# Down-projection of a ConvFFN: nine tiles by twenty-two rows of weights, or seven block products with accumulating DMAs

## The reference

```python
h = jnp.einsum('btd,de->bte', x, w_in)
# gMLP on chunks of 128, and sliding-window attention -> mix (width 1024)
mix = jnp.einsum('bte,ed->btd', mix, w_out)
x = layer_norm(DEEPNORM_ALPHA * x + mix, ln1_g, ln1_b)

up = jnp.einsum('btd,df->btf', x, w_up)                  # 1024 -> 2 * 2816
hp = jnp.concatenate([conv_prefix, up], axis=1)
hc = conv_b + sum(conv_w[i] * hp[:, i:i + T] for i in range(CONV_WIDTH))
g, u = hc[..., :D_FF], hc[..., D_FF:]
y = jnp.einsum('btf,fd->btd', jax.nn.gelu(g, approximate=False) * u, w_down)
x = layer_norm(DEEPNORM_ALPHA * x + y, ln2_g, ln2_b)
```

## Time and profile before

| | us |
|---|---|
| median of three runs | 2283.82 |
| profiled execution, span | 2283.5 |
| TensorE busy | 2185.3 (96%) |
| VectorE busy | 1651.1 (72%) |
| ScalarE busy | 981.5 (43%) |
| GpSimd busy | 832.3 (36%) |
| up-projection of a layer, by the trace | 421.5 |
| down-projection of a layer, by the trace | 268.4 |

### The profile page before, as it was taken

One profiled execution on the slowest core, in us unless ns is written; L12 is line 12 of the kernel. 1 busy time (PEld: TensorE's weight loads), 2 busy tenths in 40 slices (PEclk: granted clock), 3 DMA queues, 4 the chain that ended last, 5 costly groups with the idle time before them and its releaser, 6 DMA issues.

```text
span 2283.5 us, 35524 instructions
## 1 busy us (share of the span) xinstructions
PE 2185.3 (96%) x14132; PEld 1986.4 (87%) x14132; DVE 1651.1 (72%) x2004; ACT 981.5 (43%) x1767; POOL 832.3 (36%) x444
## 2 busy tenths in 40 slices
PE   7999999899999999999999999989999999999996
PEld 7997677799999998888899876779999999988885
DVE  1477767878788886787636687677777878867677
ACT  3226755544344434343422276464434443443342
POOL 1115255554554450320311242446455445311311
PEclk9999999999999999999999999999999999999998
DMA  6303166223322325665562122641332233365762
GB/s 157 86 20 84 33 206 175 65 58 86 88 69 77 86 69 203 235 213 195 193 140 48 48 51 87 179 152 51 83 86 77 69 88 86 98 250 185 241 217 92
DMA packets 208766, 269.74 MB, mean 118 GB/s; under 512 B 31953, under 2 KB 167377, under 8 KB 208529
## 3 DMA queue, kind: packets, MB, share of 16 engines
q1 hardware_dynamic: 208600, 267.46, 39.2%
HBM read 217.65 MB, written 46.13 MB: 116 GB/s over the span
## 4 chain that ended last, share of the span: by engine, by line
PE 76%; DVE 14%; ACT 5%; issue 3%; POOL 2%; DMA 0%; SPq 0%; ACTq 0%; DVEq 0%; POOLq 0%
PE ps L2153 37%; PE ps L1872 17%; PE ps L1831 9%; PE ps L2092 5%; DVE bnst L1292 1%; PE ps L1897 1%; DVE rl L1491 1%; PE ps L1976 1%; DVE rzc L1278 1%; PE ps L1955 1%; DVE cb L1564 1%; POOL bl L762 1%; PE ps L1991 1%; DVE Sb L1610 1%; PE ps L2002 1%
## 5 line engine op out<-in xcount | busy, mean ns | idle before, releaser
L2153 PE MATMUL ps<-bt,bh 128*128 128x272 f32 (+1 forms) x3520 | 591.1, 290 | 18.7 <-DVE bt L1397 9.3
L2153 PEld LDWEIGHTS ps<-bt,bh 128*128 128x128 f32 x3520 | 503.3, 190 | 20.3 <-DVE bt L1397 9.7
L979 ACT ACTIVATE bh<-wblk 128x512 fp32r<-128x512 f32 x308 | 183.6, 624 | 483.1 <-POOL wblk L774 268.2
L2153 PE MATMUL ps<-bt,bl 128*128 128x272 f32 (+1 forms) x1760 | 369.1, 290 | 0.0
L2153 PEld LDWEIGHTS ps<-bt,bl 128*128 128x128 f32 x1760 | 278.4, 190 | 0.0
L762 POOL TENSOR_TENSOR bl<-wblk,bh 128x512 fp32r<-128x512 f32 x98 | 168.4, 1721 | 283.8 <-ACT bh L979 283.8
L1872 PE MATMUL ps<-rh,ah 128*128 128x512 f32 x792 | 245.6, 391 | 4.6 <-DVE ah L1502 3.2
L1872 PE MATMUL ps<-rl,ah 128*128 128x512 f32 x792 | 244.1, 389 | 0.0
L2153 PE MATMUL ps<-ba,bh 128*128 128x272 f32 (+2 forms) x1408 | 233.8, 288 | 4.0 <-DVE gu L1438 2.4
L1415 DVE TENSOR_TENSOR bl<-wblk,bh 128x512 fp32r<-128x512 f32 x210 | 169.0, 837 | 91.7 <-ACT bh L979 91.7
L1491 DVE TENSOR_TENSOR rl<-wrow,rh 128x1024 fp32r<-128x1024 f32 x132 | 189.5, 1437 | 42.5 <-ACT rh L1035 42.3
(11 more groups left out here) (222 smaller groups left out, 4042.3 us busy)
## 6 DMA issues: line engine op xcount, KB each, us to landing
wrow<-in_w_down SPq DMA_DIRECT2D x132, 512.0 KB, 4.8
wblk<-in_w_up SPq DMA_DIRECT2D x88, 512.0 KB, 5.3
a_scr<-hg SPq DMA_DIRECT2D x44, 552.0 KB, 3.5
araw<-a_scr SPq DMA_DIRECT2D x88, 192.0 KB, 4.4
wrow<-in_w_out SPq DMA_DIRECT2D x48, 256.0 KB, 5.1
wrow<-in_w_out SPq DMA_DIRECT2D x24, 512.0 KB, 4.2
wraw<-in_w_in SPq DMA_DIRECT2D x10, 1024.0 KB, 6.3
z_scr<-rzc SPq DMA_DIRECT2D x16, 512.0 KB, 4.6
```

The lines of the kernel that those rows point to most:

```text
L979: act.activation(bh[b][:], block_of(f, b), ACT.Copy).then_inc(S["u_hi"], 1)
L2153: e = nc.tensor.matmul(up_half(f, b, n), lhs, rhs[:, c:HW_] if n else rhs[:, 0:c], start=(k == 0 and m == 0), stop=(k == HK - 1 and m == 2))
```

## The change

The down-projection becomes seven block products too. The 2816 inner rows are split by parity of their 128-row block (even blocks are "1", odd ones "2"), the output columns into two halves of 512, the prompt tokens into tiles 0..3 and 4..7. Seven products (`P_1, P_2, P_3, P_6, P_5, P_7, P_4`, in that order of time) of 11 steps each, NST = 77 steps in all; a step has one 128 x 512 block of weights or of a sum of weights, one 128 x 512 block of activations or of a sum, and four token tiles in four PSUM banks. The 64 samples are not part of that: for them four ordinary block products go along with P_1, P_2, P_3 and P_5, two matmuls a step.

- Sums of activations are made in the up-projection, in device memory: ScalarE writes the negated first half of `hg` (`negated`, behind `tap_up`), SyncE stores it to `e_scr` and `f_scr` (`neg_out`), and GpSimd adds to it by accumulating DMAs, of 512, 512 and 256 KB for each pair of steps (`act_add`).
- Sums of weights: blocks of `w_down` are held whole in SBUF (`w11`, `w12`, `w21`, `w22`); ScalarE negates one (`weight_neg`) and GpSimd accumulates the other onto it from device memory (`weight_add`), 12 DMAs of 0.75 to 1 MB in a layer.
- Residual rows and gains: scaled by GpSimd (`residual`), the bias row, the first product and the partial sums then accumulated by DMAs (`residual_add`, seven in a layer, of 0.25 to 2 MB); for six tiles the second layer norm's last addition is an accumulating DMA too (`gained` of GpSimd).
- Joins: VectorE adds each finished bank to the rows in SBUF (`join`, `second`, `sample_part`).
- The buffers `hg[0]` and `hg[1]` are read by those DMAs, and `tap_gate` waits for them.
- In the second layer the input projection's chunks are 512, 288 and 288 columns instead of 384, 384 and 320, and tiles 4 to 7 are transposed there instead of 6 to 8.

The core of the diff:

```diff
@@ constants
+KP = FT // 2
+NP = 7
+NST = NP * KP
+P_1, P_2, P_3, P_6, P_5, P_7, P_4 = range(NP)
+PX, PY, PZ = [6, 7, 2, 5], [3, 4, 0, 1], [2, 5, 6, 7]
+KGRP = [(0, 4), (4, 8), (8, KP)]
+X_AT = {62: 0, 64: 1, 68: 2, 70: 3, 72: 8}
@@ SyncE
+            def neg_out(l, k, which):
+                sp.wait_ge(S["neg"], neg_a(l, k, which) + 1)
+                if which == 0:
+                    sp.dma_start(e_scr[k, :, 0:3:2, :], hx[:, 0:1, :].to_broadcast([P, 2, HT])).then_inc(S["e_out"], 16)
+                else:
+                    sp.dma_start(f_scr[k], hx[:, 1, :]).then_inc(S["f_out"], 16)
...
                 sp.dma_start(a_scr[f], hg[f % 2][:]).then_inc(S[f"a_out{f % 2}"], 16)
+                if f % 2 == 0:
+                    sp.dma_start(e_scr[f // 2, :, 1, :], hg[0][:, HT:2 * HT]).then_inc(S["a_out0"], 16)
...
+                    if f >= 2:
+                        neg_out(l, f // 2 - 1, f % 2)
...
+                for s in range(4, NST):
...
+                    elif s in (14, 16):
+                        if s == 14:
+                            sp.wait_ge(S["adds1"], 16 * KP * (l + 1))
+                        z_back(l, s // 2 - 3 + (s - 14) // 2)
+                        z_back(l, s // 2 - 2 + (s - 14) // 2)
...
+                    elif s == 17:
+                        down_block(l, "w22", 0, 0, KP)
...
+                    act_block(l, s)
@@ GpSimd
+            def act_add(l, k, i):
+                n = l * KP + k
+                if i == 0:
+                    pool.wait_ge(S["e_out"], 16 * (n + 1))
+                    pool.dma_start(e_scr[k, :, 0:3:2, :], hg[0][:, HT:2 * HT].unsqueeze(1).to_broadcast([P, 2, HT]),
+                                   accum_op=ALU.add).then_inc(S["adds0"], 16)
+                elif i == 1:
+                    pool.wait_ge(S["prod"], l * FT + 2 * k + 2)
+                    pool.wait_ge(S["a_out0"], 32 * (n + 1))
+                    pool.wait_ge(S["adds0"], 16 * (n + 1))
+                    pool.dma_start(e_scr[k, :, 1:3, :], hg[1][:, HT:2 * HT].unsqueeze(1).to_broadcast([P, 2, HT]),
+                                   accum_op=ALU.add).then_inc(S["adds1"], 16)
+                else:
+                    pool.wait_ge(S["f_out"], 16 * (n + 1))
+                    pool.wait_ge(S["adds1"], 16 * (n + 1))
+                    pool.dma_start(f_scr[k], e_scr[k, :, 2, :], accum_op=ALU.add).then_inc(S["adds2"], 16)
+            def weight_add(l, which, g):
+                k0, k1 = KGRP[g]
+                tile, block, c = {T_1: (w11, 0, HT), T_2: (w22, 1, HT), T_3: (w12, 0, HT), T_4: (w21, 1, 0)}[which]
+                pool.wait_ge(S["neg"], neg_t(l, which, g) + 1)
+                after(pool, f"wadd{g}", 16 * (4 * l + which))
+                src = w_down[l].rearrange("(k two p) n -> two p k n", two=2, p=P)[block][:, k0:k1, c:c + HT]
+                pool.dma_start(tile[:, k0:k1, :], src, accum_op=ALU.add).then_inc(S[f"wadd{g}"], 16)
...
                 for f in range(1, FT):
                     lo_up(l, f, B_11)
                     lo_up(l, f, B_12)
-                    for b in SUMS:
+                    for b in SUMS[:3]:
                         sum_up(l, f, b)
+                    sum_up(l, f, B_S3)
+                    if f >= 5 and f % 2:
+                        act_add(l, (f - 5) // 2, 2)
+                    if f >= 3 and f % 2:
+                        act_add(l, (f - 3) // 2, 0)
+                    elif f >= 4:
+                        act_add(l, (f - 4) // 2, 1)
@@ ScalarE
             def tap_gate(l, f):
                 n = l * FT + f
                 act.wait_ge(S["up_in"], n + 1)
                 if f >= 2:
-                    act.wait_ge(S[f"a_out{f % 2}"], 16 * (l * (FT // 2) + f // 2))
+                    if f % 2:
+                        act.wait_ge(S["a_out1"], 16 * (l * KP + f // 2))
+                        act.wait_ge(S["adds1"], 16 * (l * KP + f // 2))
+                    else:
+                        act.wait_ge(S["a_out0"], 32 * (l * KP + f // 2))
+                        act.wait_ge(S["adds0"], 16 * (l * KP + f // 2))
...
+            def negated(l, k, which):
+                act.wait_ge(S["prod"], l * FT + 2 * k + which + 1)
+                after(act, ("adds0", "f_out")[which], 16 * (l * KP + k))
+                act.activation(hx[:, which, :], hg[which][:, 0:HT], ACT.Copy, scale=-1.0).then_inc(S["neg"], 1)
...
                     tap_gate(l, f)
                     tap_up(l, f)
+                    if f:
+                        negated(l, (f - 1) // 2, (f - 1) % 2)
+                for s in range(NST):
+                    if s + 2 < NST:
+                        down_hi(l, s + 2)
+                        act_hi(l, s + 2)
...
+                    elif 58 <= s < 63:
+                        if s < 62:
+                            deviation2(l, TOP[s - 58])
+                        if s == 61:
+                            deviation2(l, NB)
+                        normal2(l, TOP[s - 58])
@@ TensorE
+                    for m, (lhs, rhs) in enumerate(((lh_, rh_), (lh_, rl_), (ll_, rh_))):
+                        e = nc.tensor.matmul(ps[:, P_BANKS[p][i], :], lhs, rhs, start=(fresh and m == 0), stop=(final and m == 2))
...
+                    for m, rhs in enumerate((dh[s % 3], dl[s % 3])):
+                        e = nc.tensor.matmul(ps[:, P_SAMP[p], :], smp[:, f, :], rhs[:], start=(k == 0 and m == 0),
+                                             stop=(k == KP - 1 and m == 1))
```

More of the change, by code:

```diff
@@ L1073, in body @@
                 else:
-                    for t in G3[2]:
+                    for t in range(4, NB):
                         x_hi(l, t)
@@ new lines, in sample_part @@
+            def sample_part(l, n, half, bank):
+                k = JOINS * l + (J_S1 + (0 if half else 2), J_S2, J_S3, J_S5)[n]
+                dve.wait_ge(S["d_samp"], 4 * l + n + 1)
+                rz = half_of(NB, half)
+                dve.wait_ge(S["radd"], 16 * (RADDS * l + R_8))
+                if n:
+                    dve.wait_ge(S["joins"], JOINS * l + {1: J_S1 + 4, 2: J_S1 + 2, 3: J_S3 + 2}[n])
+                for i in range(2):
+                    if i:
+                        dve.wait_ge(S["joins"], k + 1)
+                    dve.tensor_tensor(rz, rz, ps[NS * i:NS * i + NS, bank, :], ALU.add).then_inc(S["joins"], 1)
@@ new lines, in second, with stats @@
+            def second(l, i):
+                dve.wait_ge(S["d_tile"], 4 * (l * NP + P_6) + i + 1)
+                dve.wait_ge(S["radd"], 16 * (RADDS * l + R_P1))
+                dve.tensor_tensor(p1[:, i, :], p1[:, i, :], ps[:, PY[i], :], ALU.add).then_inc(S["joins"], 1)
+            def stats(l, t, half):
+                q = tokens(t)
+                if t == NB:
+                    dve.wait_ge(S["joins"], JOINS * l + (J_S5 if half else J_S2) + 2)
+                else:
+                    j = (J_VT if half else J_C11) if t < 4 else J_C22 if half else J_C21
+                    dve.wait_ge(S["joins"], JOINS * l + j + t % 4 + 1)
+                dve.bn_stats(out=bst[0:q, t, 6 * half:6 * half + 6], in_=half_of(t, half)).then_inc(S["ln_bn"], 1)
@@ new lines, in body @@
+                    if l < DEPTH - 1 and s in X_AT:
+                        x_lo(l + 1, X_AT[s])
+                for t in (4, 5):
+                    join(l, J_C21, t - 4)
+                    stats(l, t, 0)
+                    moments2(l, t)
+                scaled2(l, 4)
+                scaled2(l, 5)
+                dve.wait_ge(S["gain_landed"], 64 * (l + 1))
+                gained(l, 4)
+                for t in (6, 7):
+                    join(l, J_C21, t - 4)
+                    stats(l, t, 0)
+                    moments2(l, t)
@@ new lines, in down_step @@
+                def down_step(s, tiles=(0, 1, 2, 3)):
+                    p, k = divmod(s, KP)
+                    if p in P_SAMP and k == KP - 1:
+                        down_samples(s)
+                    for i in tiles:
+                        down_tile(s, i)
+                    if p in P_SAMP and k < KP - 1 and 3 in tiles:
+                        down_samples(s)
+                down_ready(0)
+                down_step(0, (0, 1))
+                down_ready(1)
+                down_step(1, (0, 1))
@@ new lines, in body @@
+                for s in range(2):
+                    down_step(s, (2, 3))
+                for s in range(2, NST - 3):
+                    down_ready(s)
+                    down_step(s)
+                    if s == 4:
+                        rows_turn(NRB - 1)
+                    if l < DEPTH - 1 and s in X_AT:
+                        turn_x(l + 1, X_AT[s])
+                for tiles in ((0, 1), (2, 3)):
+                    for s in range(NST - 3, NST):
+                        down_ready(s)
+                        down_step(s, tiles)
```

899 lines of the change are left out of this document (593 added, 306 removed), and 2 rows, old and new, of the table S.

## The result

The changed kernel takes 2560.86 us (median of four runs, 2555.66 to 2561.84), the kernel before 2283.23 beside it: the ratio is 1.120, with a 95% interval of 1.118 to 1.122. The forecast was 2358 with a range to 2450. The direction was right, the size was not: 278 us more instead of 74. The page of the kernel after, to be read beside the earlier trace rows: span, busy times, two of the DMA queues (q0 holds the transfers issued by GpSimd, the accumulating ones among them), and the chain that ended last.

What follows compares the result with a forecast made beforehand. TensorE was taken to bound both stages, with the gate tap's new wait binding the up-projection after the change: 2283.5 - 60 + 108 + 26 = 2357.5, with 0.3 us for the median 2358 us, range 2245 to 2450.

Steps and rivals of the forecast that it cites:

- Matmuls, -60 us: Down-projection: 1012 matmuls a layer instead of 1144, at 0.2268 us each, 29.9 us a layer less on TensorE.
- a few hundredths: TensorE's granted clock in the up-projection: the most it was expected to fall, hidden because TensorE no longer bounds the loop.
- The wait of the gate tap, +108 us: Up-projection: 19 taps a layer wait for an accumulating DMA; a step lasts 19.1 + X instead of 20.97 us.
- I take 4.8 us as the mean, the load's row: the two reads and the write overlap: Up-projection: an accumulation was priced like a 512 KB load, within bounds of 3.0 and 8.8 us.
- X: Up-projection: time from issue to landing of the accumulating DMA that the gate tap waits for, taken as 4.8 us.
- issued just before: Up-projection: a second accumulation of 256 KB precedes the awaited one in every other step; no separate cost was given.
- rival 2: Up-projection: accumulations are slow, 7 us or more on the mean; with X = 8, 2479 us; chance 0.12.
- The rest of the down-projection, +26 us: Down-projection: three delays of 4 us a layer, 3 at the layer boundary, -1 for the tail; ends 5 and 90.
- Block w22: SyncE's queue, down-projection: 2.9 MB ahead of step 17's activations takes 8.6 us; 0 to 10 us, taken as 4.
- rival 3: Down-projection bound by DMA, an accumulated byte costing twice a plain one: 32 us a layer, 2398 us; chance 0.12.
- GpSimd's accumulations: Down-projection: those of 1 to 2 MB, due at steps 22, 33 to 41 and 44, cost 4 us.
- Steps 58 to 62: Down-projection: ScalarE waits for VectorE's statistics of five tiles, 3.6 us a turn against 2.72; about 4 us.

Runs made afterwards that it cites:

- e5: Changed kernel with accumulation addends read from device memory, normalisation one step later, and the bias row added by GpSimd instead of accumulating DMAs: 2351.06 us.
- e11: e8 with five closing multiplications also moved to VectorE and every accumulating DMA made a plain copy, sums left out: 2261.84 us, ratio 0.990.
- e7: e5 with the down-projection's loads reordered: w22 in pieces, w12, residual tiles and gains later, weight differences' copies and accumulations behind: 2326.70 us.
- e8: e7 with the residual tiles' multiplication and bias addition moved from GpSimd to VectorE, one tile in a step: 2292.24 us, ratio 1.0034.

## Why the prediction was wrong

By its own steps:

- **Matmuls, -60 us.** The count is right, and a matmul at full clock costs what it did. It doesn't show in the time of this kernel, since TensorE waits: in the down-projection 51 of 306 us. Its busy time there is 254.9 us, where 1012 matmuls make 229.5, and other work 7 (266.5 - 1144 x 0.2268 in the earlier trace rows): 236.5. The 18 us between fit the clock, 0.92 in this stage and 0.78 in its first hundred microseconds. The prediction allowed "a few hundredths", hidden. In the up-projection (0.94) the step is set by the tap's wait, so they are hidden; how much of the 18 us lengthens the down-projection no run shows.
- **The wait of the gate tap, +108 us.** It measures 197. Place, count (38) and formula are right. The step that failed is "I take 4.8 us as the mean, the load's row: the two reads and the write overlap". The accumulation doesn't come at the price of one load: it lands in 7.0 us (median), where a plain copy of the same bytes takes 3.7. Whether its reads and its write stand behind one another no trace shows. Measured from the sum's end X is 5.9 us for it alone, 1.1 more than the 4.8. The second part of the miss is the 256 KB accumulation "issued just before", which the prediction named and put at nothing: it turns 5.9 into 8.6 in every other step. That makes 7.2 on the mean, and each part is about half of the 89 us that were missed. The mean step of layer 0 from the second tap (459.30) to the twenty-first (963.07) is 26.5 us, and 19 x (26.5 - 20.97) - 2 = 103 us; the stage starts 103 us later. This is rival 2, X of 7 or more, which had 0.12, at a price of 229 (with X = 8) for both layers.
- **The rest of the down-projection, +26 us.** It measures about 141 (2364.2 - 2283.5 + 60), with an upper end of 90; all but a few microseconds of it stand in the down-projections. Three terms were mis-sized and one was missing:
  - *Block w22*: "full speed is near 335 GB/s and w22 takes 8.6 us". It lands in 33.2 us. The estimate gave it the whole of DMA, while accumulations and other loads shared it. The next issue on SyncE, a load of activations, takes 22.67 us (first view below), and ScalarE waits up to 12 us for the activations queued behind. That is the mechanism of rival 3, an accumulated byte at twice a plain one, but in the first hundred microseconds and not over the whole stage, whose share is 0.84. The rival took the mean of a stage with a crowded start (1.06) and emptier stretches (0.56 right behind it).
  - *GpSimd's accumulations*: "0 to 25 us, I take 4". One of 1 MB takes 9.1 to 24.3 us in the down-projection (medians by target); what their lateness costs by itself no run separates.
  - *Steps 58 to 62*: 4 us a layer, where TensorE idles 7.3 of the 29 us at 1217.
  - *Missing*: VectorE's splits counted with their mean of 0.84 us. Beside GpSimd's multiplications they take up to 2.9 us, three to four times as long. It could have been read in the kernel before (the second view below).

The issue of w22 (step 17) and the next one, in the timeline of SyncE in the kernel after:

```profile
1048.77 2.10 SPq L630 DMA_DIRECT2D w<-in_w_down  x1
1050.97 22.67 SPq L646 DMA_DIRECT2D araw<-a_scr  x1
```

And the stretch from 920 to 940 in the kernel before:

```profile
920.00:940.00 20.00, 20.00 (x90) 16.57 (x89) 19.89 (x10) 7.00 (x11) 15.79 (x6) 1.00 0.71 249
```

In that stretch, too, VectorE is full with ten instructions beside GpSimd, but TensorE works all 20 us. The buffers of one kernel cover it and those of the other, at 2.7 us a step, don't; that the shorter step is the reason is argued, not shown. And here is the same in the kernel after, at the normalisation: 2.54 us beside GpSimd, 0.68 alone.

```profile
1226.07 2.39 POOL L1049 TENSOR_TENSOR rz_top<-rz_top,gain 128x1024 f32<-128x1024 f32 x1 [7.13 <-ACT rz_top L1399]
...
1226.48 2.54 DVE L1914 TENSOR_TENSOR dl<-w,dh 128x512 fp32r<-128x512 f32 x1 [1.83 <-ACT dh L1366]
...
1228.94 0.68 DVE L1918 TENSOR_TENSOR al<-araw,ah 128x512 fp32r<-128x512 f32 x1
```

Put together from the kernels, in this order: 2560.9 minus 197 for the wait, 3 for the normalisation's place (not clear of the spread), 35 for the order of the loads together with e5's edit, 39 for products on GpSimd (half of which e5 had put there), is 2287; minus 26 for the doubled price of the remaining accumulations, 2262. The other 38 us to the ideal of 2224 (2283.5 - 60) are not taken apart by a run. By the trace of e11 some 32 of them stand in the two down-projections: they last 255.7 and 249.4 us, where 268.6 and 263.9 less 29.9 each would be the ideal. In layer 0 TensorE idles 14.8 us of it, and is busy 240.86 us at a clock of 0.98, against 236.5.

The range was too narrow because two rivals, 2 and 3, were treated as exclusive. They have one cause, the cost of an accumulated byte. If it is high, both hold, and with the two at their own prices, 229 + 26 + 40, the prediction's own numbers give 2519 us. Against the runs that has the tap's wait 32 us too long and the rest 75 us too short; contention between GpSimd and VectorE is in no rival.

## What to carry to other kernels

An accumulating DMA is no free adder: here its bytes cost twice, in landing time and in DMA share. Don't let a buffer in the inner loop be its source when a copy of the data lies in device memory, and price every transfer issued ahead of the one that is waited for. Price a burst of loads by the queue at its place in the stage and not by the stage's mean share. Before work is taken off TensorE, look at stretches in which VectorE is full with few instructions: GpSimd's operations hold it up there, and what hid that may be what is removed. Change one thing in an edit: e5 removed bytes and added GpSimd work, and the two can't be told apart. When two rivals hang on the same unknown number, add them up.

## What the runs showed of the hardware

- Accumulating costs the DMA engines twice a plain copy (17.7% and 8.8% of their time for 74.98 MB), with the target in device memory as with the target in SBUF (512 KB: 7.0 and 3.7 us; 1 MB under load: 16.6 and 7.9).
- A multiplication of 128x1024 costs 1.2 us on VectorE and 2.4 to 2.8 on GpSimd beside VectorE's splits, and on GpSimd it holds up a split by about 2 us besides (2.85 instead of 0.68). Moving nine of them and nine additions a layer to the busier engine made the kernel 34 us faster (e7, e8).
- A load issued by SyncE behind one of 2.8 MB, at a DMA share of 1.07 to 1.08, took 22.67 us to issue, and the 2.8 MB landed in 33.2 us.
- The granted clock was 0.78 in the hundred microseconds in which TensorE worked 61, 0.67 and 0.91 in two stretches with 13.6 of 20, and 0.99 where it worked 49.2 of the next 50. In the down-projection of the kernel after TensorE is busy 254.9 us with work that makes 236.5 at the kernel before's price of a matmul; its matmuls record 0.39 us (median), the slowest 0.80.
